# Two modulation rows of a two-block transformer kernel, summed by ScalarE and GpSimd in place of TensorE

## What is computed

```python
c_act = jax.nn.silu(c)
for l in range(DEPTH):                                   # first block, DEPTH = 2
    mod = c_act @ w_ada[l] + b_ada[l]
    sh1, sc1, g1, sh2, sc2, g2 = jnp.split(mod, 6, axis=-1)
    h = modulate(rms_norm(x, norm1_g[l]), sh1, sc1)
    ...
def adaln_params(cond, w, bias):                         # second block, for c and for c_ctx
    m = jax.nn.silu(cond) @ w + bias
    return jnp.split(m[..., None, :], N_MOD, axis=-1)
```

## Time and profile before

| | |
|---|---|
| time of three runs | median 2198.92 us (2196.89 to 2201.01) |
| the profiled execution | 2195.35 us, span 2193.6 us |
| PE busy | 2099.5 us, 96% |
| DVE, ACT, POOL busy | 993.0, 711.0, 276.5 us |
| moved by DMA | 657.35 MB, mean 300 GB/s |

### The profile page before, as it was taken

How to read it: one execution, slowest core, us unless ns; L and a number is a source line. 1 busy time by engine, 2 the same in 40 slices (tenths; PEclk the granted TensorE clock), 3 DMA queues, 4 the chain that set the end, 5 groups by cost and what they waited for, 6 DMA issues and landing times.

```text
span 2193.6 us, 30907 instructions
## 1 busy us (share of the span) xinstructions
PE 2099.5 (96%) x13135; PEld 1417.9 (65%) x13135; DVE 993.0 (45%) x1930; ACT 711.0 (32%) x1295; POOL 276.5 (13%) x141
## 2 busy tenths in 40 slices
PE   6999999999989999999999999899998999999999
PEld 4687784445434558877644444454764799978997
DVE  4466652222212237576322221221346587757776
ACT  3434421111101144453222111111213555566554
POOL 3554520000000035455000000000000000000000
PEclk9999999999999999999999999999999999999999
DMA  9966669999999997567799999999556285245550
GB/s 350 340 221 222 258 269 407 421 421 421 421 420 421 421 349 253 209 232 306 288 421 417 421 421 421 420 421 411 173 191 236 96 274 182 97 139 192 174 195 35
DMA packets 193594, 657.35 MB, mean 300 GB/s; under 512 B 12923, under 2 KB 116837, under 8 KB 131880
## 3 DMA queue, kind: packets, MB, share of 16 engines
q1 hardware_dynamic: 190784, 651.74, 76.6%
q0 software_dynamic: 1184, 2.08, 0.3%
q10 hardware_dynamic: 1480, 1.45, 0.2%
HBM read 654.17 MB, written 1.06 MB: 299 GB/s over the span
## 4 chain that ended last, share of the span: by engine, by line
PE 82%; DMA 9%; DVE 5%; ACT 1%; issue 1%; SPq 1%; POOL 1%; DVEq 0%; ACTq 0%; POOLq 0%
PE ps L410 80%; DMA ring<-in_w_expert_in 5%; DMA hT<-in_w_expert_in 1%; DMA ring<-in_w_in 1%; DMA HB<-in_w_expert_out 1%; SPq L677 1%; DMA AR<-in_w_ada 1%; DVE AR L762 1%; PE ps L2086 1%; DVE ARr L1687 0%; DMA wr<-in_w_router_expert 0%; PE ps L2760 0%; PE ps L2582 0%; PE ps L1999 0%; POOL cols L522 0%
## 5 line engine op out<-in xcount | busy, mean ns | idle before, releaser
L410 PE MATMUL ps<-ring,AR 128*64 128x512 f32 (+2 forms) x1952 | 530.7, 580 | 14.1 <-DMA ring<-in_w_expert_in 6.9
L410 PE MATMUL ps<-XLr,HBr 128*128 128x256 f32 x1280 | 369.7, 289 | 5.1 <-DVE XLr L889 2.1
L410 PE MATMUL ps<-hTr,ringr 128*128 128x256 f32 x1280 | 362.1, 283 | 0.0
L410 PE MATMUL ps<-hTr,HBr 128*128 128x256 f32 x1280 | 362.0, 283 | 0.0
L410 PEld LDWEIGHTS ps<-ring,AR 128*64 128x64 f32 (+1 forms) x1952 | 183.7, 141 | 268.8 <-issue 249.1
L393 POOL TENSOR_TENSOR ringr<-ring,HBr 128x1024 fp32r<-128x1024 f32 x106 | 258.8, 2459 | 732.8 <-ACT HBr L387 732.6
L410 PE MATMUL ps<-AR 128*128 128x128 f32 (+6 forms) x1928 | 329.1, 327 | 5.4 <-DVE AR L2030 2.8
L387 ACT ACTIVATE HBr<-ring 128x1024 fp32r<-128x1024 f32 x260 | 265.7, 1050 | 184.8 <-PE ps L410 157.4
L410 PEld LDWEIGHTS ps<-AR 128*128 128x128 f32 (+2 forms) x1928 | 220.3, 181 | 90.0 <-issue 69.0
L410 PEld LDWEIGHTS ps<-XLr,HBr 128*128 128x128 f32 x1280 | 245.3, 192 | 23.2 <-issue 13.5
L410 PEld LDWEIGHTS ps<-hTr,ringr 128*128 128x128 f32 x1280 | 245.4, 192 | 2.4 <-issue 1.4
(11 more groups left out here) (322 smaller groups left out, 2727.9 us busy)
## 6 DMA issues: line engine op xcount, KB each, us to landing
ring<-in_w_expert_in SPq DMA_DIRECT2D x151, 1024.0 KB, 19.8
ring<-in_w_expert_out SPq DMA_DIRECT2D x77, 1024.0 KB, 18.1
ring<-in_mod_w SPq DMA_DIRECT2D x48, 1024.0 KB, 6.8
ring<-in_ffn_w_up SPq DMA_DIRECT2D x44, 1024.0 KB, 5.2
ring<-in_w_in SPq DMA_DIRECT2D x40, 1024.0 KB, 5.4
ring<-in_w_ada SPq DMA_DIRECT2D x40, 1024.0 KB, 7.6
HB<-in_w_expert_in SPq DMA_DIRECT2D x33, 1024.0 KB, 20.8
HB<-in_w_expert_out SPq DMA_DIRECT2D x23, 1024.0 KB, 18.3
```

The source lines that it names most:

```text
L410: return pe.op.matmul(out_, lhsT, rhs, start=start, stop=stop, **kw)
```

## The change

The rows (2,2) and (3,0) are taken out of PE's and SP's list. POOL loads all tiles from (2,2) on (32 of them) on its own DMA queue, into the four slots 5, 6, 7 and 11. Beside the heads ACT multiplies each of the 16 tiles of the two rows in place by its condition values (a scalar for each partition), POOL adds tile k - 1 into tile k, for k = 1 to 7, in two halves, and PE sums the last tile over its partitions with four matmuls with ones (`pe_row`). Row (2,2) is summed behind the norm of head (2,1), row (3,0) at the end of the heads. The remaining 80 tiles keep their order on PE; the first mixer (l = 0) does 24 instead of 32, the second mixer 32 and the attention 16 as before. In `pe_heads` the projections of pair 1 are split into halves with the ropes between them.

```diff
+        MODS_LATE = (5, 6, 7, 11)
...
         def pool_program(pool):
...
+            pool_late(pool)
...
+        ROWS_AHEAD = ((2, 2), (3, 0))
...
+        late_tiles = [t for t in all_tiles if t[:2] > (2, 1)]
...
+        def pool_late_load(pool, n, r, k):
+            name = ("mod", n, r, k)
+            pool.wait_ge(*slots.free(*name))
+            src = MODS[n][0][k * 128:(k + 1) * 128, r * 2048:(r + 1) * 2048]
+            pool.op.dma_start(mod_chunk(n, r, k), src).then_inc(*late_in[late_at[name]].inc(*name))
+
+        def pool_late(pool):
+            for t in late_tiles[0:3]:
+                pool_late_load(pool, *t)
+            for i, t in enumerate(row_tiles):
+                if t[2]:
+                    pool_row_tile(pool, *t)
+                pool_late_load(pool, *late_tiles[i + 3])
+            for t in late_tiles[len(row_tiles) + 3:]:
+                pool_late_load(pool, *t)
...
+        def act_row_tiles(act, count):
+
+            for n, r, k in next_mods("rows", count):
+                name = ("mod", n, r, k)
+                w, c = mod_chunk(n, r, k), ctile[:, 8 * MODS[n][2] + k:8 * MODS[n][2] + k + 1]
+                act.wait_ge(*dve_pro["cw"])
+                act.wait_ge(*landed(name))
+                act.op.activation(w, w, ACT.Copy, scale=c).then_inc(*act_row.inc(*name))
+
+        def pool_row_tile(pool, n, r, k):
...
+            pool.wait_ge(*act_row[name])
+            if k > 1:
+                pool.wait_ge(*pool_row[before])
+            for half in (slice(0, 1024), slice(1024, 2048)):
+                pool.op.tensor_tensor(w[:, half], w[:, half], v[:, half], ALU.add).then_inc(*pool_row.inc(*name))
+            slots.until(before, pool_row, *name)
+
+        def pe_row(pe, n, r):
...
+            pe.wait_ge(*pool_row[name])
+            w = mod_chunk(n, r, 7)
+            for j in range(4):
+                t = mm(pe, b[32 * j:32 * j + 32, :], C("ones", 0, 32), w[:, j * 512:(j + 1) * 512], True, True)
...
@@ pe_mixer (dve_mixer and sp_mixer alike) @@
             pe_fm(pe, ("qk", l, 1), *X, (dve_mix, "qk", l, 1))
-            pe_mods(pe, 1 - l)
             pe_z(pe, l, m)
-            pe_mods(pe, 1)
+            pe_mods(pe, l)
             for g in range(2):
                 pe_tm(pe, ("v", l, g), *X, (dve_mix, "v", l, g))
-                pe_mods(pe, 1)
+                pe_mods(pe, l)
             pe_cum(pe, l, m)
             if l == 0:
-                pe_mods(pe, 1)
                 pe_cols(pe, 1, NR)
             pe_dproj(pe, l, X, 0, 0)
-            pe_mods(pe, 1)
+            pe_mods(pe, l)
             pe_keys(pe, l, m, 0)
             pe_mods_turn(pe)
-            pe_mods(pe, 1 if l == 0 else 0)
             pe_dproj(pe, l, X, 0, 1)
             pe_mods(pe, 1)
             pe_keys(pe, l, m, 1)
-            pe_mods(pe, 1 if l == 0 else 0)
             pe_dproj(pe, l, X, 1, 0)
...
@@ pe_heads @@
-            pe_mods(pe, 2)
             pe_projq(pe, 0, 0, norm)
...
             pe_hnorm(pe, m, 2, 1)
-            pe_mods(pe, 1)
+            pe_row(pe, 2, 2)
+            pe_projkv_half(pe, 1, 0, 0)
             pe_rope(pe, m, 1, 0)
-            pe_mods(pe, 1)
+            pe_projkv_half(pe, 1, 0, 1)
             pe_rope(pe, m, 2, 1)
-            pe_projkv(pe, 1, 0)
-            pe_mods(pe, 1)
+            pe_mods_turn(pe)
+            pe_projkv_half(pe, 1, 1, 0)
             pe_rope(pe, m, 1, 1)
-            pe_projkv(pe, 1, 1)
-            pe_mods(pe, 1)
+            pe_projkv_half(pe, 1, 1, 1)
             pe_rope(pe, m, 3, 1)
+            pe_row(pe, 3, 0)
@@ act_heads @@
             norm.act_apply(act)
+            act_row_tiles(act, 3)
             act_hsquare(act, m, 0, 0)
             act_hroot(act, m, 0, 0)
             act_hsquare(act, m, 0, 1)
+            act_row_tiles(act, 1)
             act_projkv(act, m, 0, 1)
             act_hroot(act, m, 0, 1)
+            act_row_tiles(act, 2)
             act_hsquare(act, m, 2, 0)
             act_hroot(act, m, 2, 0)
+            act_row_tiles(act, 2)
             act_hsquare(act, m, 2, 1)
             act_hroot(act, m, 2, 1)
+            act_row_tiles(act, 3)
             act_projkv(act, m, 1, 0)
+            act_row_tiles(act, 4)
             act_projkv(act, m, 1, 1)
+            act_row_tiles(act, 1)
...
@@ sp_program @@
-            sp_mods(sp, 2)
+            late_slots()
             sp_attention(sp)
             series()
-            sp_out(sp, 0, 0, 1)
-            sp_mods(sp, 1)
...
-            sp_mods(sp, 14)
+            sp_out(sp, 0, 0, 4)
             sp_ffn(sp, 0, 0, 12)
```

94 lines of the change are left out of this document (51 added, 43 removed).

## The result

The changed kernel takes 2225.73 us (median of four runs, 2225.29 to 2229.24) against 2198.95: ratio 1.0117, 95% interval 1.0102 to 1.0132, or 26.8 us slower. The prediction was slower by 6.5 us, with 2218 as the top of its range. The sign was right, the size was not.

The account below looks back on a forecast made before the run. PE, busy 96% of the span, was taken as the bound, with the expert stage DMA bound. Mixer -9, seam +1.5 and heads +14 gave +6.5 us on 2198.9, so 2205.4 us, range 2191 to 2218.

Parts of the forecast that it names:

- Mixer, -9 predicted: First mixer: eight tiles fewer on PE, with one row turn fewer, take 9 us off, bounds 5 and 12.
- the tile before z: First mixer: removing it gains 0.3 us, since PE then waits about 3.1 us for the small router weights.
- Seam, +1.5 predicted: Between expert stage and heads: POOL's four loads delay the last expert weights by 1.5 us, ends 0 and 5.
- the 15% of the earlier trace: Seam: POOL's queue moved 0.57 of 3.86 MB with engines full; that share would add 0.8 us.
- The half that I estimated: Seam: with engines alternating round robin between two full queues, each gets half, costing 4.8 us.
- Heads, +14 predicted: Attention heads: 14 us longer, with logits 11.5 us late from row waits and 2.5 us from POOL and DVE hindering each other.
- PE's side up to the logits: Heads: eight tiles leave and two row products come in; without new waits PE is through 6.7 us sooner.
- The port: Heads: POOL's additions and DVE's two-input operations slow each other, costing 2.5 us, range 0 to 6.
- Parts 1 to 3 of the prediction: The terms for first mixer (-9 us), seam (+1.5 us) and heads (+14 us).
- The queue takes half, and the port keeps DVE away: Rival: seam 4.8 us, DVE's ropes and norms 2.2 us late each, heads 19, mixer -7; 2216 us, chance 0.12.
- the mixer gives little: Rival: stalls close the first mixer's gaps, gain 5 us; 2209 with heads 14, near 2204 with heads 9; no separate chance.
- POOL keeps up: Rival: in the heads the row waits nearly vanish, costing 0 to 3 us; 2193 us in all, chance 0.16.

Follow-up runs that it names:

- a_mix: The changed kernel with two of the first mixer's tile loads issued behind the first key weights in SP's list; ratio 1.0110 to the kernel before.
- a_act: The changed kernel with ScalarE's scalings of the late tiles moved earlier in its order; ratio 1.0062 to the kernel before, 12.1 us below the changed kernel.
- a_gap: The changed kernel with GpSimd waiting for its own first half addition before the second half of each tile; a single execution, 2228.72 us.
- a_best2: The changed kernel with slot, seam, row-order, PSUM, scaling-order and semaphore repairs, a gap between GpSimd's halves and VectorE's subtractions later; 2188.72 us, 0.9940 of the kernel before.

## Why the prediction missed, point by point

Against the means over all traces (26.5 us in all), the predicted 6.5 us were short by 20: the feed-forward by 9.6, the seam by 5.4, the mixer by 4.5, experts and rest by 1.0, and the heads were over by 0.5.

- **Mixer, -9 predicted, -3.1 on the two profiled executions, -4.5 over all traces.** The step that failed is the one on the tile before z, "since the landing hardly moves". The last of the small loads landed 1.0 to 2.6 us later than in the earlier trace rows in the nine traces with this mixer, and after the wait PE ran slower as well, 3.78 us for 1.98. The prediction took that wait's end as fixed. Why it moved is argued, not shown: with SP's list shorter, four of its 1 MB loads go out between 45.8 and 47.7 us, just as POOL issues the router weights, where before it was one; the router weights took 9.7 us to land (8.5 to 9.1 in the eight others) in place of 7.6. But in a_mix, where two of the four go out later, they still took 8.6. The other terms were right in their sum: with the landing out of the way the tiles give 7.9 us, of 8.9 worked out.
- **Seam, +1.5 predicted, +7.8 measured.** The term as it was set out, the last expert weights, was right (scatter 1.6 us later). The step left out whose transfer is next on the same queue: the key and value weights, for which SP's list had been waiting for the same engines. The range's end of 5 was too low, too. The share of POOL's queue was 4.19 of 9.7 MB, 43%, not the 15% of the earlier trace rows, where that queue had only 0.57 MB to send. The half that I estimated from the Trainium skill's round robin ("DMA: Bandwidth & Descriptors", SWDGE vs HWDGE vs iDMA) was nearer to this than my row.
- **Heads, +14 predicted, +14.4 measured up to the attention's end, +15.0 up to the first logits.** Waits 5.08 and 12.96 against 6 and 12; PE's side up to the logits -6.8 against -6.7; an addition 2.36 to 2.47 us a half against 2.46. So the path through the rows was right, and that the total came so close is partly luck. The port was mis-sized: 2.5 us, as a slowing of POOL by some per cent and one or two waits for VectorE of 2.2 us, from the earlier trace rows. It is an exclusion of up to 5.5 us an operation, and it didn't show because the row waits lay over it. What stands in its place in the sum is the slower PE after each wait: 0.9 us on the row product and 2.1 on the projection half, 3.0 behind a wait of 5.08, with a granted clock of 0.50 from 1615 to 1620 us.
- **Feed-forward, nothing predicted, +10.1 measured.** The largest miss. Parts 1 to 3 of the prediction went through what PE, POOL and the queues do, and never through the turn table, although the diff takes 32 turns out of it and every later load on slots 5, 6, 7 depends on its count.
- **Rivals.** "The queue takes half, and the port keeps DVE away" (2216, chance 0.12) was the nearest: both halves of it happened. Its heads of +19 were too much, since port and rows overlap. Its point of decision, a share above a third, was met. In the mixer it was "the mixer gives little" that came about (5 us there, 4.5 over all traces). "POOL keeps up" was excluded by ScalarE's order, which a_act shows to cost 12 us, and by the port.
- **Range.** It held all the bounds of known terms and nothing for a stage that the change touches only by bookkeeping.

## What to carry to other kernels

When a change takes entries out of a list that hands out buffers in rotation, look at every later user of the rotation: a shift by one slot cost 10 us here, in a stage that the change doesn't touch. A wait in the trace names what ended last, and under it there may be others of nearly the same length (here three deep), so before moving the waiting step, ask when the next thing would be ready. And a count over several loads should hold only what its first reader reads.

## What the runs showed of the hardware that I had not expected

- VectorE's operations with two SBUF operands stand still while GpSimd adds (up to 5.54 us for 0.69; four subtractions 11.56 for 4.62), past the end of one GpSimd instruction if the next follows at once; with one operand in PSUM they take 0.69. One with a single tensor operand was held too (a_best2, L2728, 1.95 us for 0.49), the reciprocals were not (3.35 us beside additions and without).
- PE after a wait of 3 to 5 us: the same eight matmul records 1.93 us for 1.06, a projection half 9.18 for 7.07, 32 matmuls 10.19 for 7.07. The granted clock was 0.50 from 1615 to 1620 us and 0.81 from 1545 to 1550. The price is not a fixed one: in a_gap, behind a wait of 5.78 us, the same half took 7.78 us, with a granted clock of 0.61 from 1615 to 1620.
- With both DMA queues full (1520 to 1545 us), GpSimd's queue moved 43% of the bytes.
